# Running sums of the stick-breaking attention: the total carried by one product with rows of ones, and new orders of steps

## The reference

```
z = einsum(q, k) * HEAD_DIM ** -0.5                       # float32
neg_log_1m_beta = where(visible, softplus(z), 0)
between = cumsum(neg_log_1m_beta, reverse) - neg_log_1m_beta
weights = where(visible, exp(log_sigmoid(z) - between), 0)
out = weights @ v
```

## Time and profile before

| | us |
|---|---|
| median of 3 runs | 918.1 (917.25 to 918.97) |
| the profiled execution | 915.49 |
| its span, first to last instruction | 913.7 |
| PE busy | 881.7 (96%) |
| DVE busy | 470.4 (51%) |
| ACT busy | 410.1 (45%) |
| POOL busy | 65.6 (7%) |
| mean granted PE clock | 0.995 |

### The profile page before, as it was taken

One profiled execution on the slowest core, in us unless ns is written; L12 is line 12 of the kernel. 1 busy time (PEld: TensorE's weight loads), 2 busy tenths in 40 slices (PEclk: granted clock), 3 DMA queues, 4 the chain that ended last, 5 costly groups with the idle time before them and its releaser, 6 DMA issues.

```text
span 913.7 us, 19005 instructions
## 1 busy us (share of the span) xinstructions
PE 881.7 (96%) x8257; PEld 729.6 (80%) x8257; DVE 470.4 (51%) x634; ACT 410.1 (45%) x572; POOL 65.6 (7%) x84
## 2 busy tenths in 40 slices
PE   4899999999999999999999999999999999999997
PEld 3899999876877788776787887888888888888886
DVE  5348767436676745636566554444444444422243
ACT  5335554449878765664354432233333222221231
POOL 1011212011010101022200000000000000000000
PEclk9999999999999999999999999999999999999999
DMA  9231223321111112131276512333333332232221
GB/s 286 81 93 56 84 70 93 115 72 37 37 38 38 38 50 60 38 127 47 69 215 210 174 47 85 99 92 92 92 92 92 92 92 92 93 115 93 93 93 69
DMA packets 109150, 83.34 MB, mean 91 GB/s; under 512 B 2910, under 2 KB 99464, under 8 KB 108824
## 3 DMA queue, kind: packets, MB, share of 16 engines
q1 hardware_dynamic: 109080, 82.29, 29.6%
HBM read 76.51 MB, written 5.77 MB: 90 GB/s over the span
## 4 chain that ended last, share of the span: by engine, by line
PE 91%; DVE 3%; ACT 2%; issue 1%; DMA 1%; SPq 0%; POOL 0%; POOLq 0%; DVEq 0%; ACTq 0%
PE psum L554 48%; PE psum L1747 17%; PE psum L1498 9%; PE psum L1535 6%; PE psum L1672 2%; PE psum L1403 1%; PE psum L1682 1%; PE psum L1790 1%; PE psum L1653 1%; PE psum L1701 1%; DMA w_raw<-in_w_in 1%; ACT w_hi L539 1%; DVE w_lo L544 1%; PE psum L1394 1%; PE psum L1464 0%
## 5 line engine op out<-in xcount | busy, mean ns | idle before, releaser
L554 PE MATMUL psum<-h_hi,w_hi 128*128 128x512 f32 (+1 forms) x736 | 233.6, 353 | 6.8 <-DVE w_lo L544 5.1
L554 PE MATMUL psum<-h_lo,w_hi 128*128 128x512 f32 (+1 forms) x736 | 231.1, 349 | 0.0
L554 PE MATMUL psum<-h_hi,w_lo 128*128 128x512 f32 (+1 forms) x736 | 229.9, 348 | 0.0
L554 PEld LDWEIGHTS psum<-h_hi,w_hi 128*128 128x128 f32 x736 | 129.3, 189 | 28.2 <-DVE w_lo L544 5.7
L544 DVE TENSOR_TENSOR w_lo<-w_raw,w_hi 128x1024 fp32r<-128x1024 f32 x69 | 85.4, 1238 | 127.1 <-ACT w_hi L539 127.1
L554 PEld LDWEIGHTS psum<-h_lo,w_hi 128*128 128x128 f32 x736 | 128.7, 189 | 18.8 <-issue 1.0
L554 PEld LDWEIGHTS psum<-h_hi,w_lo 128*128 128x128 f32 x736 | 129.0, 190 | 18.0
L1349 DVE TENSOR_TENSOR w_lo<-w_raw,w_hi 128x1024 fp32r<-128x1024 f32 x44 | 53.8, 1225 | 132.6 <-ACT w_hi L1026 132.6
L539 ACT ACTIVATE w_hi<-w_raw 128x1024 fp32r<-128x1024 f32 x70 | 73.8, 1055 | 79.4 <-PE psum L1747 63.0
L1026 ACT ACTIVATE w_hi<-w_raw 128x1024 fp32r<-128x1024 f32 x44 | 46.3, 1056 | 69.8 <-PE psum L554 69.8
L1747 PE MATMUL psum<-w_hi,act_hi 128*128 128x512 f32 x144 | 45.7, 389 | 0.0
(11 more groups left out here) (293 smaller groups left out, 1497.2 us busy)
## 6 DMA issues: line engine op xcount, KB each, us to landing
w_raw<-in_w_in SPq DMA_DIRECT2D x42, 512.0 KB, 3.9
w_raw<-in_w_g SPq DMA_DIRECT2D x22, 512.0 KB, 3.7
w_raw<-in_w_u SPq DMA_DIRECT2D x22, 512.0 KB, 3.7
w_raw<-in_w_d SPq DMA_DIRECT2D x22, 512.0 KB, 3.5
w_raw<-in_w_out SPq DMA_DIRECT2D x8, 512.0 KB, 5.5
kept_gates<-gate_raw SPq DMA_DIRECT2D x10, 256.0 KB, 2.7
sig_t<-kept_gates SPq DMA_DIRECT2D x10, 256.0 KB, 3.0
x_in<-in_x SPq DMA_DIRECT2D x4, 512.0 KB, 6.4
```

The costliest lines, as they stand in the source:

```text
L554: mm = nc.tensor.matmul(o, w[:, (w0 + i) * P:(w0 + i + 1) * P], xs[:, k, c0:c1], start=(n == 0), stop=(n == total - 1))
```

## The change

The last product of each tile leaves in row 0 of the bank the total over this tile and all later ones. DVE copies that row, rounded, to row 0 of a new tile `carry` (`ch`), and the remainder to its row 32 (`cl`). One product of `ones_r` (ones in rows 0 and 32, zeros elsewhere) with `carry` opens the bank anew (start=True) with the total in all rows, and the triangle products of the next tile add to it. The two products with the strict triangle go. C now waits for both s and cl. `carry` and `ones_r` are filled by DVE before the lists begin. `carry` lies where `gate_up_w` lay, which is now loaded behind the lists, from ACT's queue. All four orders are new; in PE's, `m0.Q` is first, the gate halves come earlier, and `u0.U` stands before `s8.SA`, not last.

```diff
+        gup_at = cursor[0]
         gup = sb("gate_up_w", [P, 512])
+        fixed_at = cursor[0]
+        cursor[0] = gup_at
+        carry = sb("carry", [P, SEQ], F32R)
+        cursor[0] = fixed_at
...
+        ones_r = sb("ones_r", [P, P], F32R)
...
-                             (lora[64:P, :], aaa_up), (gup[:], gate_up)):
+                             (lora[64:P, :], aaa_up)):
...
                     act.wait_ge(mix_pe, len(MIX_PE))
+                    act.dma_start(gup[:], gate_up).then_inc(gup_in, 16)
                     act.wait_ge(eps_ok, 2)
                     s_.activation(osb_hi[:], qT[:], ACT.Copy).then_inc(osb_h, 1)
...
             v_.tensor_copy(tri_r[:], consts[:, K_TRI:K_TRI + 3 * P]).then_inc(tri_ok, 1)
+            v_.memset(ones_r[:].bitcast(F32), 0.0).then_inc(tri_ok, 1)
+            v_.memset(carry[:].bitcast(F32), 0.0).then_inc(tri_ok, 1)
+            dve.wait_ge(tri_ok, 3)
+            for r in (0, 32):
+                v_.memset(ones_r[r:r + 1, :].bitcast(F32), 1.0).then_inc(tri_ok, 1)
+            dve.wait_ge(tri_ok, 5)
...
+                    if s[:2] == "ch":
+                        j = int(s[2])
+                        c = slice(SEQ - WIDTH[j], SEQ)
+                        dve.wait_ge(mix_pe, upto(MIX_PE, "sum", h, f"C{j}"))
+                        v_.tensor_copy(carry[0:1, c], psum[0:1, CBANK, c]).then_inc(mix_dve, 1)
+                    if s[:2] == "cl":
+                        j = int(s[2])
+                        c = slice(SEQ - WIDTH[j], SEQ)
+                        dve.wait_ge(mix_dve, upto(MIX_DVE, "sum", h, f"ch{j}"))
+                        v_.tensor_sub(carry[32:33, c], psum[0:1, CBANK, c], carry[0:1, c].bitcast(F32)).then_inc(mix_dve, 1)
...
-                        pe.wait_ge(mix_dve, upto(MIX_DVE, "sum", h, f"s{i}"))
-                        for part in (sp_hi, sp_lo):
-                            t_.matmul(psum[:, CBANK, SEQ - WIDTH[i]:SEQ], tri_r[:, P:2 * P],
-                                      part[:, OFF[i]:OFF[i] + WIDTH[i]], start=False, stop=False,
-                                      skip_group_check=True)
+                        pe.wait_ge(mix_dve, last_of(MIX_DVE, "sum", h, (f"s{i}", f"cl{i}")))
+                        c = SEQ - WIDTH[i]
+                        t_.matmul(psum[:, CBANK, c:SEQ], ones_r[:], carry[:, c:SEQ], start=True, stop=False,
+                                  skip_group_check=True)
```

The ends of PE's order, and two stretches of it that are spoken of below:

```diff
-i0.A m0.Q i0.L s0.F a0.Q2 s0.RB i0.W1 i0.R0 a0.Q1 g0.G0 i0.Y1 a0.Q0 i0.W2 i0.R1 s0.T1 m1.Q h0.C3 i0.Y2 h0.C2
+m0.Q i0.A i0.L a0.Q2 s0.F s0.RB i0.W1 i0.R0 g0.G0 a0.Q1 s0.T0 i0.Y1 s0.T1 s0.T2 g0.G1 a0.Q0 i0.W2 i0.R1 h0.C3
+m1.Q i0.Y2 h0.C2 s0.Z i0.W3 i0.R2 g1.G0 i0.Y3 g1.G1 h0.C1 i0.W4 i0.R3 a1.Q2 h0.C0 i0.Y4 g2.G0 h0.C4 i0.W5 i0.R4
...
+h3.C3 g4.G0 h3.C2 i2.A i2.L s2.Z1 s2.Z g4.G1 i2.W1 i2.R0 s2.SA h3.C1 g5.G0 h3.C0 i2.Y1 s2.OUT1 s2.OUT i2.W2
...
-s8.F s8.RB h7.C4 i4.W5 i4.R4 s8.T2 a2.O s8.Z1 s8.Z i4.Y5 a3.O s8.SA g9.G1 s8.OUT1 s8.OUT u0.U
+s7.S i4.Y4 h7.C4 s8.F i4.W5 i4.R4 s8.RB a3.O s8.T2 i4.Y5 s8.Z1 s8.Z u0.U s8.SA s8.OUT1 s8.OUT
```

The start of DVE's order, and the steps around h3's totals:

```diff
-i0.x0 i0.aab m0.min s0.aak s0.arb s0.ark h0.min1 i0.x1 h0.max1 h0.hi1 h0.lo1 h0.min0 m0.max h0.s3 m0.hi i0.x2
+m0.min i0.x0 i0.aab s0.aak s0.ark s0.arb h0.min1 m0.max m0.hi m0.lo i0.x1 h0.max1 h0.hi1 h0.lo1 s0.v g0.raw
...
+h2.s0 h2.cl0 h3.max1 h3.min0 h3.hi1 s1.s i1.x4 h3.lo1 s2.aak s2.arb s2.ark h2.s4 i1.x5 h3.s3 s2.v h3.ch3 h3.cl3
+h3.max0 h3.ch2 h3.hi0 i2.aab i2.x0 h3.lo0 h3.s2 h3.cl2 g4.raw s2.decay h3.ch1 h3.s1 h4.min1 h3.cl1 g4.lo h3.ch0
```

More of the change, by code:

```diff
@@ L180 @@
[L180 to L184, removed]
@@ new lines @@
+m1.Q i0.Y2 h0.C2 s0.Z i0.W3 i0.R2 g1.G0 i0.Y3 g1.G1 h0.C1 i0.W4 i0.R3 a1.Q2 h0.C0 i0.Y4 g2.G0 h0.C4 i0.W5 i0.R4
+h1.C3 a1.Q1 i0.Y5 h1.C2 g2.G1 i1.A i1.L a1.Q0 h1.C1 s0.SA i1.W1 i1.R0 s0.OUT s0.S h1.C0 i1.Y1 g3.G0 h1.C4 i1.W2
+i1.R1 s1.F s1.RB h2.C3 g3.G1 h2.C2 i1.Y2 s1.T1 s1.T0 s1.T2 a0.O i1.W3 i1.R2 s1.Z1 s1.Z h2.C1 i1.Y3 s1.SA a2.Q2
+s1.OUT1 h2.C0 i1.W4 i1.R3 s1.OUT s1.S h2.C4 a2.Q1 i1.Y4 s2.F s2.RB i1.W5 i1.R4 a2.Q0 s2.T0 s2.T1 s2.T2 i1.Y5
+h3.C3 g4.G0 h3.C2 i2.A i2.L s2.Z1 s2.Z g4.G1 i2.W1 i2.R0 s2.SA h3.C1 g5.G0 h3.C0 i2.Y1 s2.OUT1 s2.OUT i2.W2
@@ new lines @@
+i2.R1 s2.S h3.C4 g5.G1 h4.C3 s3.F s3.RB i2.Y2 a1.O s3.T1 s3.T0 s3.T2 i2.W3 i2.R2 h4.C2 s3.Z1 s3.Z i2.Y3 s3.SA
+h4.C1 i2.W4 i2.R3 s3.OUT1 s3.OUT s3.S i2.Y4 h4.C0 s4.F i2.W5 i2.R4 s4.RB a3.Q2 h4.C4 i2.Y5 s4.T1 s4.T0 s4.T2
+a3.Q1 i3.A i3.L s4.Z1 s4.Z h5.C3 g6.G0 h5.C2 s4.SA i3.W1 i3.R0 s4.OUT1 s4.OUT s4.S i3.Y1 a3.Q0 h5.C1 i3.W2 i3.R1
+s5.F s5.RB g6.G1 s5.T0 i3.Y2 s5.T1 s5.T2 h5.C0 g7.G0 s5.Z1 s5.Z i3.W3 i3.R2 s5.SA h5.C4 g7.G1 s5.OUT1 i3.Y3
+s5.OUT s5.S i3.W4 i3.R3 h6.C3 g8.G0 s6.F s6.RB i3.Y4 h6.C2 g8.G1 h6.C1 s6.T1 i3.W5 i3.R4 s6.T0 s6.T2 h6.C0 i3.Y5
@@ L189 @@
+g9.G0 i4.A s6.Z1 s6.Z i4.L h6.C4 s6.SA i4.W1 i4.R0 s6.OUT1 s6.OUT s6.S i4.Y1 h7.C3 g9.G1 h7.C2 i4.W2 i4.R1 s7.F
+s7.RB a2.O s7.T0 i4.Y2 s7.T1 s7.T2 h7.C1 i4.W3 i4.R2 s7.Z1 s7.Z i4.Y3 s7.SA h7.C0 i4.W4 s7.OUT1 i4.R3 s7.OUT
+s7.S i4.Y4 h7.C4 s8.F i4.W5 i4.R4 s8.RB a3.O s8.T2 i4.Y5 s8.Z1 s8.Z u0.U s8.SA s8.OUT1 s8.OUT
 """)
 ORDER_ACT = order("""
-m0.z a0.z2 m0.exp i0.w1 i0.xt0 h0.exp1 a0.z1 h0.ln1 a0.z0 i0.xt1 i0.w2 m0.ln h0.exp0 h0.ln0 i0.xt2 i0.w3 s0.kh
-s0.bh m1.z g0.hi h0.w1 a1.z2 i0.xt3 i0.w4 h1.exp1 a1.z1 h1.ln1 i0.xt4 i0.w5 a1.z0 h1.exp0 s0.z h1.ln0 h0.w0
@@ L199 @@
[L199 to L202, removed]
+m0.z m0.exp a0.z2 i0.w1 m0.ln i0.xt0 h0.exp1 a0.z1 h0.ln1 s0.bh s0.kh g0.hi a0.z0 i0.xt1 i0.w2 h0.exp0 h0.ln0
+i0.xt2 i0.w3 s0.z m1.z h0.w1 g1.hi i0.xt3 i0.w4 h1.exp1 h1.ln1 h0.w0 a1.z2 i0.w5 i0.xt4 h1.exp0 h1.ln0 a1.z1
@@ new lines @@
+h1.w1 g2.hi a1.z0 s0.sa h2.exp1 i1.w1 i1.xt0 s0.out h2.ln1 h1.w0 h2.exp0 a0.wm i1.xt1 i1.w2 h2.ln0 g3.hi s1.bh
+s1.kh h2.w1 a0.o i1.w3 i1.xt2 s1.z s1.sa a2.z2 h3.exp1 h3.ln1 i1.w4 i1.xt3 s1.out a2.z1 h2.w0 i1.xt4 i1.w5
+h3.exp0 s2.bh s2.kh h3.ln0 a2.z0 s2.z h3.w1 i2.xt0 i2.w1 g4.hi s2.sa h4.exp1 h4.ln1 h3.w0 i2.w2 s2.out i2.xt1
+h4.exp0 a1.wm m1.exp h4.ln0 m1.ln g5.hi a1.o s3.kh s3.bh i2.w3 i2.xt2 s3.z h4.w1 s3.sa h5.exp1 i2.xt3 i2.w4
+s3.out h5.ln1 i2.xt4 i2.w5 a3.z2 h4.w0 s4.kh s4.bh h5.exp0 a3.z1 s4.z h5.ln0 s4.sa i3.xt0 i3.w1 h5.w1 s4.out
@@ L212 @@
[L212 to L216, removed]
@@ L217 @@
-i4.aab s6.decay h6.s1 h7.min1 s6.s h6.s0 i4.x1 s7.arb s7.aak h7.min0 s7.ark h6.s4 h7.max1 h7.hi1 h7.lo1 g8.raw
-i4.x2 h7.s3 h7.max0 s7.v h7.hi0 h7.lo0 h7.s2 g8.lo s7.decay h7.s1 i4.x3 s7.s h7.s0 i4.x4 s8.arb s8.ark s8.aak
-h7.s4 s8.v i4.x5 g9.raw g9.lo
+m0.min i0.x0 i0.aab s0.aak s0.ark s0.arb h0.min1 m0.max m0.hi m0.lo i0.x1 h0.max1 h0.hi1 h0.lo1 s0.v g0.raw
+g0.lo h0.min0 h0.s3 h0.ch3 h0.cl3 i0.x2 h0.s2 h0.ch2 h0.cl2 h0.max0 h0.hi0 h0.lo0 i0.x3 g1.raw h0.s1 h0.ch1
+h0.cl1 h1.min1 g1.lo h0.s0 i0.x4 h0.ch0 h0.cl0 h1.max1 h1.hi1 h1.lo1 h0.s4 h1.min0 h1.ch3 h1.cl3 h1.s3 i0.x5
@@ new lines @@
+h1.ch2 h1.s2 h1.cl2 h1.max0 h1.hi0 h1.lo0 i1.x0 i1.aab h2.min1 h1.ch1 h1.cl1 h1.s1 s0.decay g2.raw h1.ch0 i1.x1
+h1.s0 h2.max1 h1.cl0 h2.hi1 h2.lo1 s0.s h2.min0 h1.s4 g2.lo s1.arb h2.ch3 h2.cl3 s1.aak h2.s3 s1.ark g3.raw
+h2.s2 i1.x2 h2.max0 h2.ch2 h2.hi0 h2.lo0 h2.cl2 s1.v g3.lo h2.ch1 h2.s1 h2.cl1 i1.x3 s1.decay h3.min1 h2.ch0
+h2.s0 h2.cl0 h3.max1 h3.min0 h3.hi1 s1.s i1.x4 h3.lo1 s2.aak s2.arb s2.ark h2.s4 i1.x5 h3.s3 s2.v h3.ch3 h3.cl3
+h3.max0 h3.ch2 h3.hi0 i2.aab i2.x0 h3.lo0 h3.s2 h3.cl2 g4.raw s2.decay h3.ch1 h3.s1 h4.min1 h3.cl1 g4.lo h3.ch0
@@ new lines @@
+i2.x1 h3.s0 h3.cl0 h4.max1 h4.hi1 h4.lo1 h4.min0 h3.s4 s2.s m1.min g5.raw h4.ch3 s3.arb i2.x2 s3.ark h4.s3
+h4.cl3 s3.aak h4.max0 h4.hi0 h4.lo0 s3.v m1.max h4.ch2 h4.s2 h4.cl2 i2.x3 s3.decay h5.min1 h4.ch1 h4.s1 m1.hi
+m1.lo h4.cl1 s3.s i2.x4 h4.ch0 h4.cl0 h4.s0 h5.max1 s4.arb s4.aak s4.ark h5.min0 h4.s4 i2.x5 h5.hi1 h5.lo1 s4.v
+g5.lo h5.s3 i3.x0 i3.aab h5.ch3 h5.cl3 h5.max0 h5.ch2 h5.s2 h5.hi0 h5.lo0 h5.cl2 i3.x1 s4.decay s4.s h5.s1
+h5.ch1 h5.cl1 s5.arb s5.ark s5.aak h6.min1 g6.raw i3.x2 h6.max1 h5.ch0 h5.s0 s5.v g6.lo h6.hi1 h6.lo1 h5.cl0
@@ L220 @@
+s5.decay h6.min0 h5.s4 g7.raw i3.x3 h6.max0 h6.hi0 s5.s h6.s3 h6.lo0 g7.lo h6.ch3 h6.cl3 s6.aak s6.arb i3.x4
+h6.s2 s6.ark h6.ch2 h6.cl2 g8.raw h6.ch1 h6.s1 h6.cl1 h7.min1 g8.lo h6.s0 s6.v i3.x5 h6.ch0 h7.max1 h7.hi1
+h6.cl0 h7.lo1 i4.aab i4.x0 h7.min0 s6.decay h6.s4 i4.x1 s6.s h7.ch3 h7.cl3 h7.s3 h7.max0 h7.ch2 h7.s2 h7.hi0
+s7.aak s7.ark h7.lo0 s7.arb h7.cl2 g9.lo i4.x2 g9.raw s7.v h7.s1 h7.ch1 h7.cl1 i4.x3 s7.decay h7.ch0 h7.cl0
+h7.s0 i4.x4 s7.s h7.s4 s8.arb s8.ark s8.aak s8.v i4.x5
 """)
 ORDER_POOL = order("""
-i0.ident s0.bh a0.m3 a0.m2 s0.kh a0.m1 a0.m0 a1.m2 a1.m3 a1.m1 i1.ident a1.m0 s1.kh s1.bh a2.m3 a2.m2 i2.ident
@@ L1683, in _ @@
                                            part[:, OFF[j]:OFF[j] + WIDTH[j]], start=(j == 3 and part is sp_hi),
-                                           stop=False, skip_group_check=True)
+                                           stop=(part is sp_lo), skip_group_check=True)
                     mm.then_inc(mix_pe, 1)
```

32 lines of the change are left out of this document (11 added, 21 removed).

## The result

The changed kernel takes 924.35 us in the median (922.58 to 925.63, 6 runs), the kernel before on the same chip 918.02 (915.75 to 918.97, 6 runs). The ratio is 1.0069, with an interval from 1.0052 to 1.0086: about 6.3 us slower. The profiled execution took 925.63, its span is 923.4.

A forecast was written before the change was run, and what follows sets the result against it. The prediction took PE's own queue to bound the kernel. Its terms, -5.1 -1.15 +1.0 +1.75 +4.05 +1.65, gave +2.2 us on the median of 918.1, so 920.3, range 916.0 to 924.5.

The forecast's parts named there:

- rival 2: In the first three heads DVE becomes the bound: 0.5 more at each head, +3.5 to +4, 924; chance 0.17.
- The signs named in advance: Wait for aab about 2.2, holes of 0.6 before s8.OUT1 and 3.3 to 3.5 before y_sq's product, half clock behind.
- Products removed: In the eight heads' running sums on PE, 32 products go: -5.1 us.
- Changes of kind: In PE's order, 116 neighbours of different kind become 106: -1.15 us, bounds 0 and 2.3.
- DVE's added work: Eight short copy steps a head on DVE, 31 us in all, mainly hidden; DVE busy 156 us.
- The middle as a whole: Attention and recurrence stage between its seams: PE waits 1.0 us more, bounds 0 and 5.
- The start: Stage's start: DVE's fills and waits 1.05, m0.min first 0.7, so i0.W1 comes 1.75 later; bounds 0.9 and 2.4.
- The end: Stage's end: with u0.U ahead of s8.SA, 4.05 us is uncovered, 3.35 of it in one piece.
- One fall of the clock: Behind the new hole of 3.35 at the stage's end, one stretch at half clock: 1.65 us.
- Nothing is given back downstream: Behind the mix, no time returns; a rival had the later wait of 1.56 shrink: 916.1, chance 0.15.

The follow-up runs named there:

- e2: Changed kernel with the four fills moved from DVE to GpSimd and m0.min behind x0 and aab on DVE: 920.84 us, ratio 1.0036 to the kernel before.
- e3: Changed kernel's orders without ch and cl steps, with the kernel before's two strict-triangle products: 923.63 us, ratio 1.0055 to the kernel before.
- e4: Changed kernel's new product, copies and fills in the kernel before's orders, ch and cl right behind each s: 923.7 us, ratio 1.0075 to the kernel before.
- e1: Changed kernel with u0.U last again in PE's order, behind s8.OUT: 919.63 us, ratio 1.0015 to the kernel before.
- e5: As e4, but fills on GpSimd and ch and cl dropped (output incomplete, for time only): 915.94 us, ratio 0.9982 to the kernel before.
- e7: As e6, but gate half g5.G1 moved from between h3.C4 and h4.C3 to between s3.S and i2.Y4: 921.4 us, one execution.
- e6: Changed kernel with the edits of e1 and e2 together: 915.99 us, ratio 0.9987 to the kernel before.
- e8: As e6, but DVE does the first head's ch3, cl3 and s3 ahead of its min0: 916.55 us, ratio 0.9986 to the kernel before.

## Why the prediction went as it did

Slower was the likeliest, and the time is in the range at its upper edge (924.35 of 916.0 to 924.5). But +2.2 was forecast and +6.3 came. The upper part of the range was there for rival 2, DVE as the bound, which isn't what happened; that the time falls into it is luck. The signs named in advance came: 2.35 for aab (2.2), 0.50 and 3.48 at the end (0.6 and 3.3 to 3.5), half clock behind it. PE's busy time fell by 3.3 instead of 6, by 4.8 in e2, which has no stretch at half clock in the stage. Term by term:

- **Products removed, -5.1: right by its own count, less by PE's busy time.** 5.09 on the products themselves, 4.3 with what stands around them (e3 against e2).
- **Changes of kind, -1.15: less than half of it.** 0.5 (e3 against before, all that the order does to PE's busy time), within its bounds of 0 and 2.3. The 0.23 that I read in the earlier trace rows for going in and out of a gate unit isn't the price of every pair of changes; one row carried the whole term.
- **DVE's added work: its size right, the price of its waits too.** 153.68 busy (forecast 156). In this view of after (groups of DVE by form, 200 to 450 us: busy, mean ns, idle before) the copies on one row cost what full ones do:

```profile
L1273 DVE TENSOR_TENSOR meta_scores<-meta_scores,psum 16x512 f32<-16x512 f32 x8 | 5.5, 682 | 0.3
L1264 DVE TENSOR_TENSOR carry<-psum,carry 1x512 fp32r<-1x512 f32 x8 | 5.4, 680 | 0.3
...
L1259 DVE CAST carry<-psum 1x512 fp32r<-1x512 f32 x8 | 5.4, 674 | 0.9 <-PE psum L1709 0.7
```

  PE's waits for the carry are 0.7, for z_st and meta_scores 0.5, and the 0.5 for scores of before is gone: 0.7 more, where 1.0 was forecast. Rival 2, DVE as the bound, isn't what happened; e4 shows what it would have been.
- **The middle as a whole, +1.0: came out at 3.1.** What I left out are the "issue" holes, 2.8 instead of 0.4. The trace of before had one, of 0.4 at 311.82, and no term of the sum spoke of it. How large the term is one profile doesn't say: with PE's order as in after up to the end of the stage, e1 has 0.7 of such holes and e2 1.6, by which the middle would be 1.0 or 1.9. The other experiments have 1.1 or more, e5 in before's own order of PE the most.
- **The start, +1.75: mechanism and size right** (1.92), with 1.23 for the fills where 1.05 was forecast (the 0.1 for each of DVE's waits on itself stood in no row) and 0.56 for m0.min where 0.7 was.
- **The end, +4.05: right.** 3.48 for the square (forecast 3.35), 0.50 for sa (0.6), in it 0.39 for the DMA that ACT issues (0.4, which no row of before showed). e1 brings back 3.0 of these 4.0 and the fall; 0.98 for z and sa stays.
- **One fall of the clock, 1.65: its size right, their number wrong.** (The size was half of the 3.30 us of its row; the counts beside it, 9 products and 15, would give some 1.3.) Behind the hole of 3.48 the clock is at 0.50. From the first variance product to the unit before which PE waits 1.56, it is 30.91 before (404.01 to 434.92) and 32.63 after (412.22 to 444.85): 1.72. But the same holds for the start, where the hole is 2.57 between starts: the window from 208 is at 0.50, and e2, without that hole, hasn't it. I had used the row of 553.11, a fall behind 1.66, for the end and not for the start, whose hole I had myself put at 2.2. That is the step that failed most plainly: 1.7. And two rows were too few to read the clock from. The trace of before has two more holes of that size, with the clock at 1.00 behind both:

```profile
492.50 0.72 PE L1747 MATMUL psum<-wo_hi,merged_hi 128*128 128x512 f32 x2 [1.70 <-DVE wo_lo L544]
532.70 1.09 PE L1394 MATMUL psum<-consts,z_tok 128*128 128x128 f32 x8 [1.79 <-DVE z_tok L1317]
```

- **Nothing is given back downstream: right.** This wait of 1.56 stands in after as it did before:

```profile
444.85 0.51 PE L565 MATMUL psum<-h_hi,w_hi 128*128 128x512 f32 x1 [1.56 <-DVE w_lo L555]
```

With the terms as measured (products and what is around them, order, middle, start, end, fall at the start, fall at the end): -4.3 - 0.5 + 3.1 + 1.9 + 4.0 + 1.7 + 1.7 = +7.6. The stage and what follows differ by 5.80 + 1.5 = 7.3 in the two profiles, and the medians by 6.3. That last microsecond lies within what the "issue" holes alone differ by: with e1's 0.7 of them the sum would be +5.5, with e2's 1.6 it would be +6.4. What the median execution has of them, and of the falls, stays open, since only one execution of each kernel has a profile.

The Trainium skill's rule, in "TensorE: Matmul & The Clock Gate", section "HAM oscillation — how this bites in real kernels", is that idle gaps between bursts take PE back to half rate. The traces agree with it at both seams (holes of 3.48 and 2.35, both followed by 0.50). Which hole does it, the ten traces answer in part. From 60 us on, all five holes of 2.35 us and more were followed by a fall (in e3 the clock fell within the hole). Of 34 between 1.64 and 1.81, 11 were; of the ten of 1.56, one in each kernel, none. In that middle band the place counts for more than the size: the hole of 1.66 at 553 to 564 was followed by a fall in eight kernels of ten, the one of 1.8 at 532 to 543 in two, the one of 1.7 at 492 to 503 in none, e7's of 1.64 was, and e4's of 1.72 and 1.78 and e5's of 1.74 were not. And in e6 two small ones, 0.48 and 0.50 a microsecond apart, were followed by a fall, which in e1, e7 and e8 they were not. By these counts a fall belongs in the sum behind each new hole of 2.35 us or more, and with a chance of about a third behind one of 1.6 to 1.8; between 1.81 and 2.35 there is no case. I had put one behind the largest alone.
